# Attention probabilities of two mixers turned on VectorE in 32 x 32 blocks and through DRAM, instead of on TensorE

## The reference, cut to what matters

```
z = rmsnorm(x) @ w_in[l]            # cut into moba, fox, forget, latents, dilated
o_moba = moba_attention(qa, ka, va) # with 256 rows and one block: plain causal softmax attention
o_fox  = causal attention with a forget-gate bias
o_mla  = causal attention on latents (192 and 128 wide) projected up
o_dil  = dilated_mixture(qd, kd, vd) # softmax weights over three windows, as one weighted softmax
y = concat(o_moba, o_fox, o_mla, o_dil) @ w_out[l];  x = x + rmsnorm(y)
x = x + rmsnorm(swiglu(rmsnorm(x)))
```

## Time and profile before

| | |
|---|---|
| median of 3 runs | 1740.65 us (1740.37 to 1742.47) |
| span of the profiled execution | 1738.6 us |
| PE busy | 1728.0 us, 99% of the span |
| DVE busy | 1222.5 us, 70% |
| ACT busy | 928.7 us, 53% |
| granted TensorE clock | 9 (90% or more of full speed) in each of the 40 slices |

### The profile page before, as it was taken

The page is one execution under the profiler, slowest core; times in us unless marked ns, Lnnn a source line. Parts: engine busy times, 40 slices in busy tenths (PEclk is TensorE's granted clock), DMA queues, the critical chain, the costliest instruction groups (busy, mean ns, idle before and its releaser), DMA issues.

```text
span 1738.6 us, 22208 instructions
## 1 busy us (share of the span) xinstructions
PE 1728.0 (99%) x8141; PEld 1434.5 (83%) x8141; DVE 1222.5 (70%) x1583; ACT 928.7 (53%) x1438; POOL 102.6 (6%) x257
## 2 busy tenths in 40 slices
PE   8999999999999999999999999999999999999998
PEld 7888888888888888888888888888888888888887
DVE  8977656888666766567976766676656797676665
ACT  6665445666544554455564554455445556455443
POOL 5110000201000000001000100000000100010000
PEclk9999999999999999999999999999999999999999
DMA  8548776665877678868775677777786777658773
GB/s 268 154 148 252 232 227 209 187 182 161 244 231 224 211 239 253 251 207 265 229 256 194 199 239 231 224 223 236 244 253 219 256 225 261 202 187 240 234 222 122
DMA packets 343516, 384.45 MB, mean 221 GB/s; under 512 B 90128, under 2 KB 273968, under 8 KB 343152
## 3 DMA queue, kind: packets, MB, share of 16 engines
q1 hardware_dynamic: 340928, 375.29, 69.0%
q0 software_dynamic: 2176, 7.75, 1.5%
q10 hardware_dynamic: 304, 0.01, 0.0%
HBM read 353.62 MB, written 29.36 MB: 220 GB/s over the span
## 4 chain that ended last, share of the span: by engine, by line
PE 95%; DVE 2%; ACT 1%; DMA 1%; POOL 1%; issue 0%; DVEq 0%; POOLq 0%; ACTq 0%
PE Dp L2263 29%; PE Gp L2263 19%; PE Tp L2263 19%; PE Dp L2231 8%; PE Dp L2232 8%; PE Dp L2233 8%; PE Dp L2283 1%; PE Gp L2471 1%; ACT Z L1218 1%; DVE wlo L1472 0%; PE Tp L2246 0%; DMA bfor<-in_b_forget 0%; PE Gp L2480 0%; DVE Z L1863 0%; PE Dp L2493 0%; DMA posi<-in_positions 0%
## 5 line engine op out<-in xcount | busy, mean ns | idle before, releaser
L1472 DVE TENSOR_TENSOR wlo<-raw,whi 128x1024 fp32r<-128x1024 f32 (+1 forms) x608 | 712.6, 1208 | 278.1 <-ACT whi L969 277.9
L969 ACT ACTIVATE whi<-raw 128x1024 fp32r<-128x1024 f32 (+1 forms) x608 | 607.6, 1045 | 377.3 <-PE Dp L2263 123.3
L2263 PE MATMUL Dp<-whi,a_hi 128*128 128x512 f32 (+1 forms) x668 | 179.7, 391 | 0.5 <-DVE a_lo L1544 0.4
L2263 PE MATMUL Dp<-whi,a_lo 128*128 128x512 f32 (+1 forms) x668 | 178.5, 388 | 0.0
L2263 PE MATMUL Dp<-wlo,a_hi 128*128 128x512 f32 (+1 forms) x668 | 177.2, 387 | 0.0
L2263 PEld LDWEIGHTS Dp<-wlo,a_hi 128*128 128x128 f32 x668 | 124.8, 188 | 25.6 <-DVE wlo L1472 0.4
L2263 PEld LDWEIGHTS Dp<-whi,a_lo 128*128 128x128 f32 x668 | 124.4, 188 | 24.9
L2263 PEld LDWEIGHTS Dp<-whi,a_hi 128*128 128x128 f32 x668 | 122.8, 188 | 26.4 <-issue 1.3
L2231 PE MATMUL Dp<-whi,b_hi 128*128 128x512 f32 (+1 forms) x364 | 144.5, 397 | 0.0
L2233 PE MATMUL Dp<-whi,b_lo 128*128 128x512 f32 (+1 forms) x364 | 141.5, 389 | 0.0
L2232 PE MATMUL Dp<-wlo,b_hi 128*128 128x512 f32 (+1 forms) x364 | 141.4, 389 | 0.0
(11 more groups left out here) (287 smaller groups left out, 2219.5 us busy)
## 6 DMA issues: line engine op xcount, KB each, us to landing
raw<-in_ffn_w_gate_up SPq DMA_DIRECT2D x176, 512.0 KB, 5.0
raw<-in_w_in SPq DMA_DIRECT2D x132, 512.0 KB, 4.9
raw<-in_ffn_w_down SPq DMA_DIRECT2D x88, 512.0 KB, 4.4
raw<-in_w_gate SPq DMA_DIRECT2D x44, 512.0 KB, 4.0
raw<-in_w_up SPq DMA_DIRECT2D x44, 512.0 KB, 5.1
raw<-in_w_down SPq DMA_DIRECT2D x44, 512.0 KB, 4.5
held<-Z SPq DMA_DIRECT2D x132, 128.0 KB, 4.4
Z<-held SPq DMA_DIRECT2D x132, 128.0 KB, 4.7
```

Of the source, the lines that this page charges most:

```text
L969: return nc.scalar.activation(whi[g % W][0:rows, c0:c0 + n], raw[g % R][0:rows, c0:c0 + n], ACT.Copy).then_inc(hi_done, 1)
L1472: return V.tensor_tensor(wlo[g % W][0:rows, c0:c0 + n], raw[g % R][0:rows, c0:c0 + n], whi[g % W][0:rows, c0:c0 + n].bitcast(F32), ALU.sub ...
L2263: return mm(bank, a[:, 4 * h + k, tile(t)], w[g % W][:, n * k:n * k + n], start=start, stop=stop, skip_group_check=True)
```

## The change

The probabilities of M0, M1, D0 and D1 are no longer turned by PE. DVE transposes them in 32 x 32 blocks (`turn_probs`), into `trail` for tile 0 and into `inner` for tile 1; SP stores them in DRAM (`store_p`) and fetches them back (`fetch_p`), and `values` multiplies straight from what was fetched. `turn_p` and `p_out` of these four items go. L0, F0, L1 and F1 are turned by PE as before. ACT instead of DVE copies the keys of M1 and D0. `values` of these items stands later in PE's order: M0 behind the scores of D0, M1 behind `chunk(0, FQ0, 1, 6)`, D0 before the scores of L0, D1 behind OUT_D and with its result in another bank (`T(1)`). `heads_hi` and `heads_lo` move with them. The semaphores `blocked`, `stored` and `fetched` of the feed-forward parts are shared, so their counts are offset (`sent_p`, `sent_f`); this adds no instruction.

```diff
@@ -600,6 +640,21 @@
                 sp.dma_start(mla_k(t).rearrange("p (q n) -> p q n", q=4),
                              held_qk[1].rearrange("(q c) (b n) -> (c b) q n", q=4, b=3)).then_inc(qk_in[n], 16)
 
+            def store_p(l, n):
+                t = ITEM[n][1]
+                i = sent_p(l, n)
+                sp.wait_ge(blocked[t], i + 1)
+                if i:
+                    sp.wait_ge(fetched[t], 16 * i)
+                sp.dma_start(held_p[t], p_blocks[t]).then_inc(stored[t], 16)
+
+            def fetch_p(l, n):
+                t = ITEM[n][1]
+                i = sent_p(l, n)
+                sp.wait_ge(stored[t], 16 * (i + 1))
+                sp.dma_start(p_blocks[t].rearrange("p (q n) -> p q n", q=4),
+                             held_p[t].rearrange("(q c) (b n) -> (c b) q n", q=4, b=4)).then_inc(fetched[t], 16)
...
@@ -623,14 +678,24 @@
 
                 for l in range(LAYERS):
                     u = g - base1(l)
-                    if u == 11:
+                    if u == 8:
+                        store_p(l, M0)
+                    elif u == 10:
+                        fetch_p(l, M0)
+                    elif u == 11:
+                        store_p(l, M1)
+                        fetch_p(l, M1)
+                    elif u == 12:
+                        store_p(l, D0)
                         store_qk(l, L0)
-                    elif u == 12:
+                        fetch_p(l, D0)
                         fetch_qk(l, L0)
                     elif u == 13:
+                        store_p(l, D1)
                         store_qk(l, L1)
                     elif u == 14:
                         fetch_qk(l, L1)
+                        fetch_p(l, D1)
 
...
-                p_out(M0, l)
                 refill(b + 3)
-                heads_hi(M0, l)
                 q_turned(M1, l)
+                k_turned(M1, l)
...
                 q_turned(D0, l)
+                k_turned(D0, l)
                 softmax(M1, l)
                 refill(b + 5)
-                p_out(M1, l)
+                heads_hi(M0, l)
                 softmax(D0, l)
                 values_dil(0, l)
                 refill(b + 6)
-                heads_hi(M1, l)
-                p_out(D0, l)
-                heads_hi(D0, l)
...
                 softmax(D1, l)
+                heads_hi(M1, l)
                 values_dil(1, l)
                 refill(b + 8)
-                p_out(D1, l)
+                heads_hi(D0, l)
...
-                heads_hi(D1, l)
                 p_out(L0, l)
                 softmax(F0, l)
+                heads_hi(L0, l)
                 fox_qk(1, l)
                 refill(b + 10)
-                heads_hi(L0, l)
+                heads_hi(D1, l)
                 p_out(F0, l)
...
-                if earlier:
-                    dve.wait_ge(p_turned, 12 * l + turned_before(earlier[-1] + 1))
+                if earlier and earlier[-1] in MOVED_P:
+                    dve.wait_ge(blocked[t], sent_p(l, n))
+                elif earlier:
+                    dve.wait_ge(p_turned, TURNS_P * l + turned_before(earlier[-1] + 1))
...
+            def turn_probs(n, l):
+                t = ITEM[n][1]
+                i = sent_p(l, n)
+                dve.wait_ge(p_norm, 8 * l + n + 1)
+                if n in (D0, D1):
+                    dve.wait_ge(o_done, 8 * l + VAL[M1 if t else M0] + 1)
+                elif l:
+                    dve.wait_ge(o_done, 8 * (l - 1) + VAL[D1 if t else D0] + 1)
+                flat = probs[t].rearrange("p h s -> p (h s)")
+                V.transpose(p_blocks[t].rearrange("p (b k c) -> p b k c", b=4, c=32),
+                            flat.rearrange("p (k c b) -> p b k c", c=32, b=4)).then_inc(blocked[t], 1)
...
                 weigh(M0, l)
+                turn_probs(M0, l)
                 forget_b(l)
...
                 lo(b + 3 + W, 0)
-                k_turned(M1, l)
...
                 forget_sums(l)
-                heads_lo(M0, l)
...
                 maxima(M1, l)
-                k_turned(D0, l)
                 refill(b + 4)
                 mask(D0, l)
                 weigh(M1, l)
+                turn_probs(M1, l)
                 maxima(D0, l)
+                heads_lo(M0, l)
                 lo(b + 5 + W, 0)
-                p_out(M1, l)
                 dil_weights(D0, l)
                 dil_sums(D0, l)
                 weigh(D0, l)
+                turn_probs(D0, l)
                 lo(b + 5 + W, 1)
-                heads_lo(M1, l)
                 rotate_dil(1, l)
-                heads_lo(D0, l)
                 turn_qk(L0, l)
...
                 weigh(D1, l)
+                turn_probs(D1, l)
+                heads_lo(M1, l)
                 turn_qk(L1, l)
                 mask(L0, l)
                 maxima(L0, l)
-                p_out(D1, l)
+                heads_lo(D0, l)
...
                 lo(b + 8 + W, 1)
-                heads_lo(D1, l)
...
                 maxima(L1, l)
+                heads_lo(D1, l)
...
                 def values(n):
                     kind, t = ITEM[n]
-                    pe.wait_ge(pT_act, 8 * l + n + 1)
-                    if t:
-                        pe.wait_ge(pT_dve, 4 * l + T1_ORDER[n] + 1)
+                    if n in MOVED_P:
+                        pe.wait_ge(fetched[t], 16 * (sent_p(l, n) + 1))
+                    else:
+                        pe.wait_ge(pT_act, STAYED * l + stayed(n) + 1)
+                        if t:
+                            pe.wait_ge(pT_dve, STAYED1 * l + stayed(n, (1,)) + 1)
...
+                                h = at(n, 2 * k + j)
+                                o = value_bank(n)[HD * j:HD * j + HD, P * k:P * k + P]
+                                if n in MOVED_P:
+                                    o, p = o.rearrange("p (q s) -> p q s", q=4), p_moved(n, e, h)
+                                else:
+                                    p = pT[e][:, h, :]
+                                ins = mm(o, v_of(kind, e, 2 * k + j), p, start=e == 0, stop=e == t, skip_group_check=True)
...
@@ -2550,9 +2629,7 @@
                 turn_latents(1)
                 chunk(1, MQ0, 1, 1)
 
-                turn_p(M0)
                 chunk(0, DQ0, 1, 3)
-                values(M0)
                 pe.wait_ge(rope_m[1], 3 * l + 3)
                 pe.wait_ge(llo[1], 2 * l + 2)
...
                 pe.wait_ge(kvo[0], l + 1)
                 scores(D0)
+                values(M0)
                 values_chunk(0, DV, 5)
-
-                turn_p(M1)
                 chunk(1, DQ0, 1, 3)
+                chunk(0, FQ0, 0, 6)
+                pe.wait_ge(rope_d[1], 3 * l + 3)
+
+                pe.wait_ge(masked, 8 * l + D0 + 1)
+                turn_qk(D1)
+                ups(1)
+
+                scores(D1)
+                chunk(0, FQ0, 1, 6)
+
+                pe.wait_ge(kvo[1], l + 1)
                 pe.wait_ge(pfree[1], 7 * l + 2)
-
-                pe.wait_ge(o_lo, 8 * l + M0 + 1)
                 values(M1)
-
-                chunk(0, FQ0, 0, 6, lambda: turn_p(D0))
-
-                pe.wait_ge(o_lo, 8 * l + M1 + 1)
+                values_chunk(1, DV, 5)
+                values_chunk(0, FV, 7)
+
+                pe.wait_ge(o_lo, 8 * l + VAL[M1] + 1)
                 pe.wait_ge(pfree[0], 7 * l + 5)
                 values(D0)
-                pe.wait_ge(rope_d[1], 3 * l + 3)
-
-                turn_qk(D1)
-                ups(1)
-
-                scores(D1)
-                chunk(0, FQ0, 1, 6)
-                values_chunk(1, DV, 5)
-                values_chunk(0, FV, 7)
                 scores(L0)
-                turn_p(D1)
 
                 pe.wait_ge(pfree[0], 7 * l + 6)
                 pe.wait_ge(aug[0], l + 1)
                 turn_qk(F0)
                 chunk(1, FQ0, 0, 6)
 
-                pe.wait_ge(kvo[1], l + 1)
+                pe.wait_ge(masked, 8 * l + D1 + 1)
+                scores(F0)
+
+                turn_p(L0)
+
+                pe.wait_ge(pfree[0], 7 * l + 7)
+                out_part(0, OUT_M, M0, True, False)
+
+                pe.wait_ge(o_lo, 8 * l + VAL[D0] + 1)
+                values(L0)
+                chunk(1, FQ0, 1, 6)
+
+                scores(L1)
+                out_part(0, OUT_D, D0, False, False)
+
+                pe.wait_ge(masked, 8 * l + F0 + 1)
                 pe.wait_ge(pfree[1], 7 * l + 5)
                 values(D1)
...
```

More of the change, by code:

```diff
@@ L166, with moved_p, moved_rank, sent_p @@
 ITEM = [("moba", 0), ("moba", 1), ("dil", 0), ("dil", 1), ("mla", 0), ("fox", 0), ("mla", 1), ("fox", 1)]
-T1_ORDER = {M1: 0, D1: 1, L1: 2, F1: 3}
-T0_ORDER = {M0: 0, D0: 1, L0: 2, F0: 3}
 QK_ORDER = {M0: 0, M1: 1, D0: 2, D1: 3, F0: 4, F1: 5}
+VAL = {M0: 0, M1: 1, D0: 2, L0: 3, D1: 4, F0: 5, L1: 6, F1: 7}
 PIECES1 = [("q", L0), ("k", L0), ("q", L1), ("k", L1)]
-def build(nc, A, held, held_piece, held_qk, held_x, out):
+MOVED_P = (M0, M1, D0, D1)
+def moved_p(n):
+    return sum(1 for m in MOVED_P if ITEM[m][1] == ITEM[n][1])
+def moved_rank(n):
```

(42 more changed lines are left out.)

46 lines of the change are left out of this document (17 added, 29 removed).

## The result

The changed kernel takes 1766.64 us (median of 4 runs, 1764.24 to 1769.52), the kernel before 1740.51 us beside it (4 runs, 1739.8 to 1742.47). The ratio is 1.0149, with a 95% interval of 1.0136 to 1.0162: slower by 26 us. The forecast was 1754.0 with a range of 1746 to 1761. The sign is right and the time lies outside the range.

A forecast was written before the change was run, and what follows sets the result against it. PE was taken as the bound, with DVE nearly full in the mixers. Waits of 9.65 us less 2.7 spared gave +6.7 a layer, +13.4 in two: 1754.0 us, own range 1750 to 1758, with rivals 1746 to 1761.

The forecast's parts named there:

- What DVE gets: Transposition steps of 1.0 and 2.0 us on DVE, less copies dropped: net 4.1 us a layer against 4.6 us idle.
- one element a cycle: Rival: a 1024 wide DVE transposition has a step of 1.15 us, giving 1750.7 us; chance 0.12.
- What PE is spared: PE's turns of M0, M1, D0 and D1 fall away: 0.45 + 0.88 + 0.45 + 0.88 = 2.7 us a layer.
- DVE over 95% busy between 37 and 91 us: Sign expected in the changed trace: DVE almost full over that stretch of the first layer.
- Turn of M1's queries: M0's transposition stands ahead of M1's rotation on DVE, so PE waits 2.3 us there.
- First fox chunk, behind ACT's V eviction: At `chunk(0, FQ0, 0)`, D0's maxima and exponentials come later, ACT evicts V later, and PE waits 1.3 us.
- Its second remainder, and the turn of D1's queries: PE waits 1.8 us for the fox chunk's second remainder and 1.8 more at the turn of D1's queries.
- `values(D0)` behind `heads_lo(M1)`: PE waits 2.45 us at `values(D0)` because DVE has `heads_lo(M1)` behind D1's transposition.
- the bank wait is not there: Rival: D1's division is not late and `values(D0)` finds its bank free, giving 1749.2 us; chance 0.08.
- DRAM trips and SP at nothing: Stores, fetches and SP's queue cost nothing; if that cover goes, 1 to 3 us a layer.
- Faster: Rival: DVE takes 4.1 us into its 4.6 us idle and PE never waits, giving 1735.3 us; chance 0.08.
- The Sum: PE's waits of 9.65 us, less 2.7 spared and 0.2 rounding: +6.7 us a layer, +13.4 for two layers.

The follow-up runs named there:

- e2: The changed kernel with the four transpositions reading columns that lie side by side instead of every fourth float: 1758.21 us.
- e1: The changed kernel with unread products put into all five PE waits of each first mixer: 1755.68 us.
- e9: The changed kernel with nine unread products ahead of the turn of M1's queries only: 1759.95 us.
- e3: The changed kernel with M0's transposition moved behind `rotate_dil(0)` on DVE: 1757.12 us.
- e4: The changed kernel with all four transpositions moved later on DVE, behind what PE waits for: 1753.97 us.
- e11: The kernel before with unused DVE transpositions (one of 512 columns, four of 64) ahead of M1's rotation, and nine unread PE products: 1744.67 us.
- e5: The changed kernel with `heads_lo(M1)` ahead of D1's transposition on DVE instead of behind it: 1765.57 us.

## Why the prediction was right in its places and wrong in its size

Point by point, by the forecast's own steps:

- **What bounds the kernel.** Right: PE has no slack, and DVE hands over without any.
- **What DVE gets.** Right. The wide transposition takes 1.98 to 2.05 us (2.08 forecast), and the 512 wide one 1.08. The rival of one element a cycle falls for this pattern, though not in general: side by side columns take 1.245 us in e2.
- **What PE is spared.** 2.7 a layer forecast; no run measures it by itself. In e1 and e9, where the clock never fell in the second layer, waits and fillers less the measured step of 7.1 leave 1.8 and 2.1 for it, so it may have been put too high by 0.6 to 0.9 us a layer, and what the sum below leaves to the clock is then smaller by as much.
- **DVE over 95% busy between 37 and 91 us.** Wrong. In that stretch DVE was busy 42.98 of 53.7 us, 80%, where it was busy 49.07 before. PE waited for DVE, and DVE in turn for PE (2.87 us for M1's scores, 2.86 for D1's): it was late at the hand-overs and not full.
- **Turn of M1's queries.** 2.3 forecast, 2.23 measured.
- **First fox chunk, behind ACT's V eviction.** 1.3 and 1.22. The chain named is the one seen: maxima, four exponentials, eviction at 64.58, chunk at 65.08.
- **Its second remainder, and the turn of D1's queries.** 1.8 and 1.8; measured 1.74 and 1.46.
- **`values(D0)` behind `heads_lo(M1)`.** 2.45 and 2.16. So the rival *the bank wait is not there* falls.
- **DRAM trips and SP at nothing.** Right for the changed kernel: no wait of PE is put down to `held_p` or to weights. e3 and e4 show the price when that cover goes, 2.5 to 4.1 us a layer, above the 1 to 3 that I gave. Fetches land in 3.9 (256 KB) and 4.5 us (512 KB), near the 4.1 of the earlier trace rows; stores take 3.5 and 2.6, longer than its 2.1.
- **Faster.** DVE's new work did not go into its idle time; that rival falls.
- **The Sum. This is the step that failed.** It adds waits, takes off what PE is spared, and stops: "+6.7 us a layer". It takes every PE instruction between the waits to last as long as before. They did not: PE ran at 1.2 GHz in six stretches. In the first layer F0's turn is 13.0 us late, in the second the step is 12.6 longer; the waits less what is spared account for 5.9 to 6.0 in each, which leaves 7.1 and 6.7 to the clock, against clock losses of 8.5 and 6.8 in the windows. These 13.8 us, with the new wait of 1.2 us behind the mixers, where the forecast had "PE waits nowhere", less 1.5 us by which the waits were put too high, are the miss: 13.5 by this sum, 13.7 by the spans (1765.7 and 1752.0). Where I read 1.00 in the earlier trace rows I took it for a constant; it was a property of an engine that did not pause.

That the clock loss was caused by idle PE is shown by e1 and e11, which put products into the idle time and change nothing else. What decides whether a given wait is followed by a fall is open. Twelve kernels were profiled beside the kernel before. In their mixers the clock fell during or behind

- single waits of 2.5 to 4.1 us (the fetches of e3 and e4) 4 times in 4,
- single waits of 2.1 to 2.3 us 12 times in 15,
- of 1.65 to 1.9 us 2 times in 4, and of 1.4 us 0 times in 2,
- of 1.1 to 1.2 us 1 time in 7, and of 0.9 to 1.0 us 1 time in 7,
- the remainder of the fox chunk and D1's queries together (1.1 to 1.8 and 1.5 us, some 2 us apart) 9 times in 12,
- and never where no wait was over 0.6 us.

The 1.22 us ahead of the first fox chunk, which the changed kernel, e5 and e9 have twice each, is in none of these groups: in none of the six did the clock fall before the next wait. Ahead of the mixers the wait of 2.02 us was followed by a fall 3 times in 3.

Each profile is one execution, so these are counts and no law. Longer idle time makes a fall likelier; the length alone does not decide it.

## What to carry to other kernels

On a kernel whose TensorE is never idle, count a new wait of 2 us or more at its length and then again for the clock, here 1.7 or 3.4 us in 16 cases of 19; the profile of before cannot show this, because its clock is 1.00 throughout. Moving 2.7 us of work off the full engine lost here already by the pauses, 5.8 to 8.8 us in the second layer of every kernel with the change but e1; the clock made it worse by 1.7 to 6.8, except in the profiled execution of e9 (waits of 7.3 us, no fall in that layer). Unread products in a pause are a cheap test of it: if the kernel gets faster with more work, the clock is what is lost.
